# Prologue of a two-layer hybrid encoder kernel: modulation totals as row sums, inputs and weights laid out by the host

## The reference

```python
def adaln(c, w, b):
    mod = (c @ w + b)[:, None, :]
    shift, scale, gate = jnp.split(mod, 3, axis=-1)
    return shift, scale, gate
...
        shift, scale, gate = adaln(c, w_ada_mix[l], b_ada_mix[l])
        u = x * (1.0 + scale) + shift
        y = hybrid_mixer(u, w_in[l], ...)
        x = layer_norm(DN_ALPHA * x + (1.0 + gate) * y, ln1_g[l], ln1_b[l])
        shift, scale, gate = adaln(c, w_ada_ffn[l], b_ada_ffn[l])
        u = x * (1.0 + scale) + shift
        y = conv_gated_mlp(u, w_up[l], ffn_conv_w[l], ffn_conv_b[l], w_down[l])
        x = layer_norm(DN_ALPHA * x + (1.0 + gate) * y, ln2_g[l], ln2_b[l])
```

## Time and profile before

| | us |
|---|---|
| median of three runs | 2102.52 (2101.42 to 2104.25) |
| the profiled execution | 2101.31 |
| its span, first to last instruction | 2099.5 |
| TensorE matmul busy | 2064.8 |
| GpSimd busy | 1413.6 |
| VectorE busy | 1191.1 |
| ScalarE busy | 1031.2 |

### The profile page before, as it was taken

The page is one execution under the profiler, slowest core; times in us unless marked ns, Lnnn a source line. Parts: engine busy times, 40 slices in busy tenths (PEclk is TensorE's granted clock), DMA queues, the critical chain, the costliest instruction groups (busy, mean ns, idle before and its releaser), DMA issues.

```text
span 2099.5 us, 27374 instructions
## 1 busy us (share of the span) xinstructions
PE 2064.8 (98%) x9619; PEld 1701.8 (81%) x9619; DVE 1191.1 (57%) x1940; ACT 1031.2 (49%) x1845; POOL 1413.6 (67%) x1780
## 2 busy tenths in 40 slices
PE   7999999999999999999999999999999999999997
PEld 6877778787888878888788888888878888888887
DVE  5888888675515554777632645587651455332235
ACT  3585356555516674374643756235562465333332
POOL 4987767755778887875557885564556776545454
PEclk9999999999999999999999999999999999999999
DMA  8644544533434354553233333332323332434332
GB/s 301 157 134 148 161 127 148 162 108 103 121 111 124 107 162 145 141 159 93 76 100 106 111 111 91 101 103 73 100 76 107 88 104 84 128 99 123 94 100 78
DMA packets 421510, 250.07 MB, mean 119 GB/s; under 512 B 48149, under 2 KB 393085, under 8 KB 421373
## 3 DMA queue, kind: packets, MB, share of 16 engines
q1 hardware_dynamic: 420506, 248.03, 39.8%
q10 hardware_dynamic: 867, 0.29, 0.1%
HBM read 242.71 MB, written 4.26 MB: 118 GB/s over the span
## 4 chain that ended last, share of the span: by engine, by line
PE 86%; POOL 5%; ACT 3%; DVE 3%; issue 2%; ACTq 0%; DMA 0%; POOLq 0%; DVEq 0%
PE fg L886 27%; PE fg L888 27%; PE fg L887 27%; POOL w_lo L1932 3%; PE bank_s L984 1%; POOL ada_acc L2003 1%; ACT ada L1324 1%; PE bank_l L915 1%; PE bank_t L993 1%; PE bank_t L1006 1%; DVE bank_c L1539 0%; POOL ssum L2030 0%; POOL u_lo L2012 0%; ACT probs L1291 0%; ACT probs L1283 0%
## 5 line engine op out<-in xcount | busy, mean ns | idle before, releaser
L1932 POOL TENSOR_TENSOR w_lo<-raw,w_hi 128x256 fp32r<-128x256 f32 (+1 forms) x1425 | 1031.3, 755 | 609.8 <-ACT w_hi L1163 608.7
L886 PE MATMUL fg<-u_hi,w_hi 128*128 128x512 f32 x2112 | 834.7, 395 | 6.2 <-DVE u_lo L1519 2.6
L888 PE MATMUL fg<-u_hi,w_lo 128*128 128x512 f32 x2112 | 823.7, 390 | 0.0
L887 PE MATMUL fg<-u_lo,w_hi 128*128 128x512 f32 x2112 | 823.5, 390 | 0.0
L1163 ACT ACTIVATE w_hi<-raw 128x1024 fp32r<-128x1024 f32 (+2 forms) x387 | 375.6, 971 | 385.6 <-PE fg L888 278.4
L886 PEld LDWEIGHTS fg<-u_hi,w_hi 128*128 128x128 f32 x2112 | 397.1, 188 | 102.5 <-issue 14.5
L888 PEld LDWEIGHTS fg<-u_hi,w_lo 128*128 128x128 f32 x2112 | 397.0, 188 | 84.2
L887 PEld LDWEIGHTS fg<-u_lo,w_hi 128*128 128x128 f32 x2112 | 397.4, 188 | 80.1 <-issue 0.5
L1539 DVE SCALAR_TENSOR_TENSOR bank_c<-glu,par,bank_c 128x512 f32<-128x512 f32 x448 | 306.1, 747 | 0.1
L1886 DVE SCALAR_TENSOR_TENSOR x<-fg,mod,x 128x512 f32<-128x512 f32 (+1 forms) x168 | 121.6, 724 | 319.3 <-PE fg L888 319.0
L888 PE MATMUL fg<-h_hi,w_lo 128*128 128x512 f32 (+1 forms) x704 | 269.8, 383 | 0.0
(11 more groups left out here) (272 smaller groups left out, 1860.8 us busy)
## 6 DMA issues: line engine op xcount, KB each, us to landing
raw<-in_w_up_dram SPq DMA_DIRECT2D x176, 512.0 KB, 3.8
ada<-in_w_ada_ffn_dram SPq DMA_DIRECT2D x48, 512.0 KB, 4.4
raw<-in_w_down_dram SPq DMA_DIRECT2D x64, 384.0 KB, 3.5
raw<-in_w_in_dram SPq DMA_DIRECT2D x40, 512.0 KB, 4.0
raw<-in_w_down_dram SPq DMA_DIRECT2D x64, 320.0 KB, 3.1
ada<-in_w_ada_mix_dram SPq DMA_DIRECT2D x32, 512.0 KB, 4.2
raw<-in_w_in_dram SPq DMA_DIRECT2D x32, 256.0 KB, 3.7
raw<-in_w_out_dram SPq DMA_DIRECT2D x32, 256.0 KB, 2.9
```

Source lines behind the costliest of these rows:

```text
L886: pe.matmul(out, hi[:, k, :], rhi, start=k == order[0], stop=False)
L887: pe.matmul(out, hi[:, k, :], rlo, start=False, stop=False)
L888: ins = pe.matmul(out, lo[:, k, :], rhi, start=False, stop=k == order[-1])
L1932: ins = pool.tensor_tensor(lo_of(n)[:, ks, :], raw[n % NRAW][:, ks, :], hi_of(n)[:, ks, :].bitcast(F32), ALU.subtract)
```

## The change

The host now passes x transposed (features first), the modulation weights transposed, so that an output feature lies on a partition and the 1024 weights of that feature along its row, and takes the first block's result feature-major from a second output. With that:

- Prologue: SyncE loads slab 0, then for each feature tile k two row sets of 128x1024 (shift and scale), with slab 1 behind the first and two tiles of x behind every second. `c` is one row, spread over the partitions by two matmuls with a row of ones and copied by ScalarE to `c_rows`. VectorE makes each total in one pass, product and row sum (`first_total`). ScalarE adds the biases per tile and makes `tmp` and `u_hi` of the tile at once. The low halves of tiles 0 to 5 are GpSimd's, of 6 and 7 VectorE's.
- GpSimd's order is `split_lo(0)`, `split_lo(1)`, `angles(0)`, six low halves, `split_lo(2)`, `history`, `split_lo(3)`, `angles(1)`, clears. ScalarE's order is `split_hi(0)`, the copies of `c`, `split_hi(1)`, parameters, eight tiles, `split_hi(2)`.
- Chunks 4 to 23: GpSimd multiplies a quarter's rows by `c_rows` (two operations of 128x512), ScalarE copies 128x1024 over itself with a row sum into `mod`, one slot later and behind its other steps (`ae`). For chunks 8 to 10 VectorE does both in one pass of 128x1024. SyncE's load of quarter m waits for the end of quarter m - 2. The sums on TensorE, and the copies and reductions after them, are gone.
- All transposes of x on TensorE and of the first block's result, their copies by ScalarE and VectorE, and all idle products are gone.

```diff
-INSIDE = {("cm", 0): 2, ("cv", 0): 4, ("xm", 0): 4, ("xr", 0): 6,
-          ("as", 12): 2, ("as", 18): 2}
+INSIDE = {("cm", 0): 2, ("cv", 0): 4, ("xm", 0): 4, ("xr", 0): 6}
...
+LO_ON_POOL = 6
...
-        if c in ONES_CHUNKS:
-            at(ns[-1] + 2, "as", c)
-        else:
-            put(ns[-1] + 2, "as", c)
+        for part, n in enumerate(ns):
+            if c not in DVE_CHUNKS:
+                at(n + 1, "ae", c, part)
+        if c >= DVE_CHUNKS[0]:
+            used[ns[-1] + 2] += 7
...
     for t in range(TB, TT):
-        put(t - TB + 2, "xt", t)
+        used[t - TB + 2] += 7
...
+            def load_x(b, i):
+                sp.dma_start(x[:, 2 * i:2 * i + 2, b * T:(b + 1) * T],
+                             a["x"][2 * i * P:2 * (i + 1) * P, b * T:(b + 1) * T].rearrange("(k p) n -> p k n", p=P)).then_inc(in_x[b][i], 16)
 
             def load_first(k):
+                for half in (0, 1):
+                    sp.dma_start(first_ada[k][:, half, :], a["ada_first"][k, half]).then_inc(in_first[k][half], 16)
 
             def load_ada(m):
                 if m >= 2:
-                    sp.wait_ge(ada_add[added(m - 2)[0]], added(m - 2)[1])
+                    sp.wait_ge(*part_done(m - 2))
...
+            load_w(0)
+            for k in range(DT):
+                load_first(k)
+                if k == 0:
+                    load_w(1)
+                if k % 2 == 0:
+                    load_x(0, k // 2)
+            load_rows(rows2, rows3)
             for n in range(2, NRAW):
                 load_w(n)
-            sp.wait_ge(in_first[-1], 16)
-            load_rows(rows2, rows3)
             sp.dma_start(nsink[:], a["sinks"]).then_inc(in_sinks, 16)
-            for t in range(TB, TT):
-                load_x(t)
+            for i in range(DT // 2):
+                load_x(1, i)
             load_ada(0)
...
-                    if ns[0] == 0 and k == DT // 2 - 1:
-                        first_rest()
+                    if ns[0] == 0 and k == DT - 1:
+                        taps_turn()
...
+            for half in (0, 1):
+                pe.matmul((bank_t, bank_s)[half][:], ones_1[0:1, :], c_rows[0:1, half, :], start=True, stop=True).then_inc(set_pe, 1)
...
             def first_inputs(k):
+                act.wait_ge(first_one, 1)
+                act.wait_ge(first_sum, 2 * k + 1)
+                act.activation(bias[:, 0, k:k + 1], mod[:, 0, 0, k:k + 1], ACT.Identity,
+                               bias=par1[:, 0, OFF["b_ada_mix"] + k:OFF["b_ada_mix"] + k + 1]).then_inc(first_fold, 1)
+                act.wait_ge(first_sum, 2 * k + 2)
+                act.activation(gain[:, 0, k:k + 1], mod[:, 0, 0, DT + k:DT + k + 1], ACT.Identity, bias=scale_0[:, k:k + 1]).then_inc(first_fold, 1)
+                act.wait_ge(first_fold, 2 * k + 2)
+                if k % 2 == 0:
+                    act.wait_ge(in_x[0][k // 2], 16)
+                if k >= 2:
+                    act.wait_ge(*first_low(k - 2))
+                inputs(tmp[:, k % 2, :], xs(0, k), 0, k, iu)
                 inputs(u_hi[0][:, k, :], xs(0, k), 0, k, ihi)
...
+            def ada_total(c, part):
                 m = (c - CHUNKS_BEFORE) * QUARTERS + part
+                act.wait_ge(ada_mul, 2 * sum(ada_engine(i) == "act" for i in range(m + 1)))
+                rows = ada[m % 2][:].rearrange("p h n -> p (h n)")
+                act.activation(rows, rows, ACT.Copy, accum_out=total_of(c, part)).then_inc(ada_done["act"], 1)
...
+            def first_total(k, half):
+                dve.wait_ge(in_first[k][half], 16)
+                rows, c = first_ada[k][:, half, :], half * DT + k
+                dve.scalar_tensor_tensor(out=rows, in0=rows, scalar=1.0, in1=c_rows[:].rearrange("p h n -> p (h n)"),
+                                         op0=ALU.mult, op1=ALU.mult, accum_out=mod[:, 0, 0, c:c + 1]).then_inc(first_sum, 1)
...
+            for k in range(LO_ON_POOL, DT):
+                dve.wait_ge(iu, k + 1)
+                dve.wait_ge(ihi, k + 1)
+                dve.tensor_tensor(u_lo[0][:, k, :], tmp[:, k % 2, :], u_hi[0][:, k, :].bitcast(F32), ALU.subtract).then_inc(first_ilo["dve"], 1)
...
+            def ada_weigh(c, part):
                 m = (c - CHUNKS_BEFORE) * QUARTERS + part
+                pool.wait_ge(in_ada[m % 2], 16 * (m // 2 + 1))
+                pool.wait_ge(set_col, 2)
+                for i in (0, 1):
+                    pool.tensor_tensor(ada[m % 2][:, i, :], ada[m % 2][:, i, :], c_rows[:, i, :], ALU.mult).then_inc(ada_mul, 1)
...
-            for n in range(2):
-                split_lo(n)
-            for k in range(DT // 2):
+            split_lo(0)
+            split_lo(1)
+            angles(0)
+            for k in range(LO_ON_POOL):
                 first_lo(k)
-            angles(0)
             split_lo(2)
-            pool.wait_ge(set_pe, 4)
+            pool.wait_ge(set_pe, 5)
             for j in range(CT):
                 history(0, j)
+            split_lo(NHI)
             angles(1)
-            split_lo(NHI)
```

More of the change, by code:

```diff
@@ L380, in plan @@
     for t in range(TB):
[L381 removed]
+        at(346 + 2 * t, "tm", t)
     put(330, "rows")
@@ L403 @@
 NORM_SPANS = [("c", "m", "k", i) for i in range(len(MIXERS))] + [("x", "m", "k", i) for i in range(len(NORMS) - 1)]
-SUM_BANK = {}
-for _c in range(CHUNKS_BEFORE, 4 * NCHUNK):
-    _n, = slots(("as", _c))
-    _norm = any(min(slots((k + m, i))) <= _n <= max(slots((k + e, i))) for k, m, e, i in NORM_SPANS)
-    SUM_BANK[_c] = "t" if _norm else "l"
-FOLD_ORDER = [("half", 0), ("half", 1)] + [s[1:] for steps in STEPS for s in steps if s[0] == "fold"]
+FOLD_ORDER = [s[1:] for steps in STEPS for s in steps if s[0] == "fold"]
 FOLDED = {}
@@ L484, in build @@
         ada = [sb(f"ada{i}", [P, 2, T]) for i in range(2)]
-        ada_acc = [sb(f"ada_acc{i}", [P, T]) for i in range(2)]
+        c_rows = sb("c_rows", [P, 2, T])
         tmp = sb("tmp", [P, 2, T])
@@ L1008, in weigh_v @@
                 ins.then_inc(pv_done, 1)
-            def sum_ada(c):
-                e, adds = added((c - CHUNKS_BEFORE + 1) * QUARTERS - 1)
-                pe.wait_ge(ada_add[e], adds)
-                take(SUM_BANK[c], *copied(c))
-                out = bank_t if SUM_BANK[c] == "t" else bank_l
-                src = ada_acc[c % 2]
-                if c in ONES_CHUNKS:
-                    for i in range(TB):
-                        ins = pe.matmul(out[:, i:i + 1], src[:, i * P:(i + 1) * P], ones_1[:, 0:1], start=True, stop=True)
-                    ins.then_inc(ada_sum, 1)
-                else:
-                    turned(out, lambda i: src[:, i * P:(i + 1) * P]).then_inc(ada_sum, 1)
-            def to_tokens(t, half, out):
-                ins = transposes(out, half, lambda k: x[:, k, t * P:(t + 1) * P])
-                ins.then_inc(y_t_done, 1)
             def do(step):
@@ L1040, in do @@
                     weigh_v(*step[1:])
-                elif what == "as":
-                    sum_ada(step[1])
-                elif what == "xt":
-                    x_to_features(step[1], (bank_t, bank_s))
                 elif what == "tl":
                     tail_turn(step[1])
-                elif what == "tm":
-                    t = step[1]
-                    pe.wait_ge(xout, DT * (NORM_NO["f", 1, 0] + 1))
-                    for half in (0, 1):
-                        take("ts"[half], y_evac[half], t + 1)
-                        to_tokens(t, half, (bank_t, bank_s)[half])
             def tail_turn(part):
@@ L1337, in _ @@
+            split_hi(0)
+            for half in (0, 1):
+                act.wait_ge(set_pe, half + 1)
+                act.activation(c_rows[:, half, :], (bank_t, bank_s)[half][:], ACT.Copy).then_inc(set_col, 1)
             split_hi(1)
-            act.wait_ge(set_pe, 2)
+            act.wait_ge(set_pe, 3)
             act.activation(par1[:], fg[1][:].rearrange("p (l n) -> p l n", n=P)[:, 0:DEPTH, 0:N1], ACT.Copy).then_inc(set_par, 1)
             for k in range(DT):
-                if k == DT // 2:
-                    split_hi(2)
@@ L1394, in _ @@
                     split_hi(n + NHI)
-                for step in STEPS[n]:
+                for step in sorted(STEPS[n], key=lambda step: step[0] == "ae"):
                     what = step[0]
@@ L1419, in _ @@
                         a_hi(*step[1:])
[L1420 to L1425 removed]
+                    elif what == "ae":
+                        ada_total(*step[1:])
                     elif what in ("ch", "xh"):
@@ L1435, in _ @@
                         x_final(*step[1:])
-                    elif what == "tm":
-                        stage(step[1], bank_t)
             act.wait_ge(tail_shift, 1)
-            act.wait_ge(y_out[1], 16)
             for half in (0, 1):
@@ L1820, in background @@
                 elif what == "ad":
-                    add_ada(*step[1:])
-                elif what == "as" and step[1] not in ONES_CHUNKS:
-                    reduce_ada(step[1])
```

(7 more changed lines are left out.)

334 lines of the change are left out of this document (77 added, 257 removed).

## The result

| | before | after |
|---|---|---|
| median | 2102.8 us (2101.4 to 2104.3) | 2122.5 us (2116.6 to 2124.4) |
| the profiled execution's span | 2099.5 | 2120.2 |

The changed kernel is slower: ratio 1.0088, 95% interval 1.0076 to 1.0101. The forecast was 2097.0, its range ended at 2107.

What follows compares the result with a forecast made beforehand. GpSimd was taken to set slab 11's start, and TensorE's own work the end from there. The sum was 2101.31 + 8.9 (slab 11 later) - 13.2 (work off TensorE) = 2097.0 us, with a range of 2083 to 2107.

Steps and rivals of the forecast that it cites:

- GpSimd's multiplies in the chunks' new form: Chunks behind slab 11's start: eight multiplies for seven adds, +1.29 us a chunk on GpSimd, taken at nothing because of idle time.
- The prologue step: Prologue: VectorE's 16 passes alternate with GpSimd's instructions; low halves from 38.9, pair of slabs 0 and 1 ends at 53.2.
- the turns: Prologue: VectorE and GpSimd hold each other off for one instruction; a piece and a pass together take 1.75 us.
- rivals 1 and 2: Rival 1: no turns in the prologue, GpSimd hardly held off, 2085 us, chance 0.20; rival 2 has its own line.
- rival 3: Prologue: without idle products TensorE stays at the lower clock through the pair, +7 us, so 2104; chance 0.12.
- rival 2: Prologue: VectorE's passes with row sum run at half rate, 2.2 to 2.4 us each, so 2115; chance 0.10.
- The price off TensorE: Behind slab 11's start: the dropped result transposes (3.5 us) and chunk sums (7.0 and 2.7) take 13.2 us off TensorE.
- Slab 11: Its start, set by GpSimd's rotary product of k, which comes 8.9 us late: slab 11 starts at 118.3.
- Nothing given back: Behind slab 11's start: nothing hides or replaces the 13.2 us saved on TensorE; waits there 0 to 3 us in the range.
- rival 4: Attention stages: new waits (ScalarE on GpSimd, SyncE on ScalarE) give back 3 to 8 of the 13.2 us, 2100 to 2105; chance 0.15.

Runs made afterwards that it cites:

- e1: The changed kernel with GpSimd's second multiply of each quarter waiting for the first one's semaphore: 2104.9 us, ratio 1.0010 to the kernel before.
- e8: e1 with GpSimd's two multiplies of each quarter cut from 512 columns to one, results wrong, only for pricing: 2093.3 us, ratio 0.9962 to the kernel before.
- e4: The changed kernel with both edits, those of e1 and e2: 2101.5 us, ratio 0.9990 to the kernel before.
- e2: The changed kernel with GpSimd's low halves of the first six input tiles ahead of the angles: 2116.0 us, ratio 1.0060 to the kernel before.

## Why the prediction was wrong

The step that failed is the one on GpSimd's multiplies in the chunks' new form. The forecast counted their durations, took them "at nothing, since behind 109.50 both have idle time", and left the waits that they enter out of the sum. The runs showed 17.6 us for operations of VectorE that the multiplies shut out, and 5.2 us given back behind slab 11. A smaller miss is 2.9 us of low clock. The parts in order:

**The prologue step was right.** Forecast: passes of 1.2 alone and 1.7 beside a split, the last total at 36.4 to 37.6, low halves from 38.9, pair's end at 53.2, split of slab 4 67.6 to 70.4. VectorE's and GpSimd's timelines of after:
```profile
14.77 1.73 DVE L1331 SCALAR_TENSOR_TENSOR first_ada<-first_ada,c_rows 128x1024 f32<-128x1024 f32 x1
...
27.15 1.25 DVE L1331 SCALAR_TENSOR_TENSOR first_ada<-first_ada,c_rows 128x1024 f32<-128x1024 f32 x1
...
12.35 11.47 POOL L1748 TENSOR_TENSOR w_lo<-raw,w_hi 128x256 fp32r<-128x256 f32 x8 [11.90 <-ACT w_hi L1064]
...
33.35 1.23 POOL L1771 TENSOR_SCALAR whole<-turns 128x64 f32<-128x64 f32 x1
...
38.47 2.49 POOL L1817 TENSOR_TENSOR u_lo<-tmp,u_hi 128x512 fp32r<-128x512 f32 x2
```
From start to start a pass took 1.66 us beside a split and 1.17 otherwise, the last total came at 35.5, the first low half at 38.47, the pair ended at 53.4, the split of slab 4 ran from 66.8 to 69.6. The last total is 0.9 us earlier than forecast, since the loads didn't hold it up. So the turns are priced by the earlier trace rows to 0.1 us each, and rivals 1 and 2 are out. So is rival 3: matmuls of the pair lasted 0.63 us from 40.45 on and 0.40 from 45.40 on, and the pair still ended on time. On rival 2: the Trainium skill (Vector Engine (DVE) Microarchitecture Reference, Points that are easy to get wrong) says half the throughput for two fp32 SBUF sources; with 1.17 us for 1024 columns and the row sum the trace disagrees, and the measurement decides.

**The price off TensorE was right.** Forecast 13.2 us behind slab 11: 0.44 a chunk, 0.89 a chunk of ones passes, 0.87 a store. Matmul by matmul, e1 against before, the chunk sums that stand alone give back 0.43 to 0.45 each, each of the four transposes of the result 0.88.

**Slab 11: the mechanism right, the clock left out.** In e1, without shut-outs, GpSimd's rotary product of k ends 8.4 us late (113.82 against 105.40) for a forecast of 8.9. But I took slab 11 to be as late as that product. The wait for `kz` is 4.30 us and not 1.77, and behind it the granted clock is at the lower of its two levels (1.2 GHz). Windows of e1: the wait, behind it, and after that (the columns of the earlier trace rows; PEclk is third from the end):
```profile
112.10:116.90 4.80, 0.53 (x5) 0.29 (x3) 4.74 (x6) 3.36 (x5) 4.80 (x6) 0.94 0.80 204
116.90:122.50 5.60, 5.57 (x17) 4.80 (x18) 3.27 (x4) 0.00 (x0) 5.60 (x7) 0.50 0.03 12
122.50:126.00 3.50, 3.50 (x15) 2.82 (x15) 2.84 (x5) 1.61 (x9) 1.47 (x2) 0.91 0.00 0
```
The scores take 1.72 us from start to start instead of 0.91, and matmuls of slab 11 are 0.43 apart instead of 0.23: 2.9 us until the clock is back. So slab 11 starts at 118.65, close to the 118.3 forecast, but 2.1 of the 2.9 us come within it: from there on TensorE is 11.3 us late, not 8.9. The forecast had the cold TensorE as rival 3, but in the pair of the prologue alone.

**Nothing given back: wrong, rival 4.** From 11.3 late less 13.2 the end should be 1.9 us early. In e1 it is 3.3 us late: 5.2 us are given back. The largest piece is 3.6 us at 215, its slow matmuls included; another 1.9 are TensorE's waits for `h_lo` (waits of before, then of e1: us in total, times, longest us):
```profile
PE fg L886 <- DVE h_lo L1919: 1.3, 2, 0.7
```
```profile
PE fg L853 <- DVE h_lo L1735: 3.3, 4, 1.5
```
Smaller gains and losses make up the rest. At 215 VectorE's quarter of chunk 8 waited for its load, and TensorE for VectorE (e1, VectorE and TensorE):
```profile
209.85 1.23 DVE L1425 SCALAR_TENSOR_TENSOR ada<-ada,c_rows 128x1024 f32<-128x1024 f32 x1 [4.30 <-DMA ada<-in_ada_t_dram]
...
215.04 0.90 PE L882 MATMUL bank_l<-const,wide 128*128 128x128 f32 x4 [2.09 <-DVE wide L1419]
```
That load is the one that SyncE now issues only behind ScalarE's pass of two quarters before, which waits for GpSimd's product. I had named this chain, and left it out of the sum: the range had 0 to 3 us for such waits, and rival 4 had 3 to 8 with a chance of 0.15. The longer work of both engines I took at nothing, "since behind 109.50 both have idle time". An average idle share isn't slack at the point where an engine is wanted. e8 confirms the cause in sum: with GpSimd's multiplies cut and the order of SyncE behind ScalarE kept, nothing is given back, and the waits for `h_lo` fall to 0.7 us.

**The shut-outs: not among the cases at all, 17.6 us.** The forecast priced "GpSimd multiplies eight times per chunk for seven adds" by duration. What differs is also that the adds ran on the same accumulator, each waiting for the one before, and that the multiplies have no such wait; e1 puts it back. The Trainium skill (SBUF — State Buffer, Summary: rules for kernel authors) says of a VectorE operation with two SBUF inputs and a GpSimd operation that reads SBUF that the second to issue blocks until the first finishes. The trace agrees for every pass of the prologue. At 86.31 it doesn't: the first finished 0.54 us later, and VectorE stood for 12.91.

The account, from before's profiled span: 8.4 (GpSimd late) + 2.9 (clock) - 13.2 (off TensorE) + 5.2 (given back) = 3.3, which is e1's (2102.8 - 2099.5), and 17.4 more (after's span less e1's) makes the 20.7 of after. The 5.2 is what the other terms leave of the 3.3, so the sum has to come out; what supports it are the pieces named above and e8. The sum without shut-outs, 2104.6 on the forecast's own footing, is 7.6 above the forecast and within its range; the range had no case for the shut-outs. The chances, as their parts stand, add up to 0.35 for the same and 0.13 for slower, not 0.32 and 0.16; nothing here rests on it.

The angles ahead of the low halves, which the forecast saw as the reason for the late pair, are worth 3.4 to 4.6 us (e4). With that undone, the chain in, and the clears on VectorE, the change is a small gain: 2098.3 us, ratio 0.9983 (0.9974 to 0.9993), still short of the forecast.

## What to carry to other kernels

When work moves between two engines that hold each other off, read not only how long the new instructions are but whether they wait for one another: in this kernel VectorE was kept out for up to 13 instructions only where GpSimd's multiplies followed each other, or were followed, with no wait, and a wait of 0.1 us between two of them won 17.6 us. Behind a wait of TensorE that grows, look for slow matmuls that follow it, and add them. And where an edit puts one more engine into the chain that frees a buffer, price it at the place where that buffer is wanted next, not by the engines' idle share.

## What the runs showed of the hardware

- A VectorE operation with two SBUF inputs can be passed over by up to 13 GpSimd instructions in a row (12.91 us for an operation of 0.74). At least one boundary was missed in 11 of 33 arrivals during the first or joined `ada` multiply with no pause about it, and in none of 46 during the second. In the seven unpaused stretches of the two artificial streams with GpSimd reading SBUF twice, 6 of 170 missed one boundary, never more, and had come within 0.08 us of it.
- A VectorE pass of 128x1024 with two SBUF inputs and row sum: 1.17 us from start to start, and 0.08 us to read the sum out. In turns with 512-column GpSimd operations it takes 2.23 us (e2), with 256-column pieces 1.66 (after).
- A wait of TensorE and the clock behind it don't go together in a simple way: after TensorE had waited 4.30 and 2.09 us (e1) and 3.22 us (after), the next slab's first matmul took 0.77 to 0.80 us, the lower clock; after 2.56 us in e8 it took 0.47.
